# Order of the page, store, gate and head transfers on the issuing queue of a stick-breaking attention stage

## The reference, cut to what matters

```
z = q k^T * SB_HEAD_DIM**-0.5 + bias            # 8 heads of 64
log_keep = where(k_pos < q_pos, log_sigmoid(-z), 0)
between  = reverse_cumsum(log_keep) - log_keep
a = where(k_pos < q_pos, exp(log_sigmoid(z) + between), 0)
o = a v;   o = o * silu(gate)
```

## Time and profile before

| | us |
|---|---|
| median of 3 runs | 3360.61 (3356.51 to 3362.72) |
| the profiled execution | 3363.24 |
| its span | 3360.6 |
| `sb_prompt`, pair 0 (first product to first product of the next) | 574.9 to 670.8 |
| pair 1 | 670.8 to 772.0 |
| pair 2 | 772.0 to 872.8 |
| pair 3, to the last gating | 872.8 to 936.4 |

### The profile page before, as it was taken

How to read it: one execution, slowest core, us unless ns; L and a number is a source line. 1 busy time by engine, 2 the same in 40 slices (tenths; PEclk the granted TensorE clock), 3 DMA queues, 4 the chain that set the end, 5 groups by cost and what they waited for, 6 DMA issues and landing times. The chain is left out here.

```text
span 3360.6 us, 46161 instructions
## 1 busy us (share of the span) xinstructions
PE 2947.2 (88%) x17599; PEld 2570.9 (77%) x17599; DVE 1535.9 (46%) x1933; ACT 861.1 (26%) x1326; POOL 585.4 (17%) x504
## 2 busy tenths in 40 slices
PE   7999998987966888788888999999888998888887
PEld 7988887433436787788568999999777888888657
DVE  6276665777555673341424221111355642341423
ACT  5211113555751101220232100011232232120221
POOL 0002222554711221100011210000222301100011
PEclk9999998867987998899998999999887898989988
DMA  7379886776434002313541222222444453202641
GB/s 262 120 253 308 301 298 205 222 231 200 122 138 163 19 19 80 120 38 121 212 151 50 107 100 100 94 81 100 171 166 143 163 184 104 94 31 99 233 158 63
DMA packets 242194, 489.51 MB, mean 146 GB/s; under 512 B 37897, under 2 KB 98954, under 8 KB 241682
## 3 DMA queue, kind: packets, MB, share of 16 engines
q1 hardware_dynamic: 225298, 429.04, 38.0%
q0 software_dynamic: 12560, 43.07, 3.8%
q10 hardware_dynamic: 4176, 15.32, 1.1%
HBM read 378.83 MB, written 112.78 MB: 146 GB/s over the span
## 5 line engine op out<-in xcount | busy, mean ns | idle before, releaser
L414 PE MATMUL ps<-in_hi,w_hi 128*128 128x344 f32 x2496 | 806.4, 323 | 92.4 <-DVE in_lo L317 92.4
L415 PE MATMUL ps<-in_lo,w_hi 128*128 128x344 f32 x2496 | 803.8, 322 | 0.0
L416 PE MATMUL ps<-in_hi,w_lo 128*128 128x344 f32 x2496 | 802.8, 322 | 0.0
L414 PEld LDWEIGHTS ps<-in_hi,w_hi 128*128 128x128 f32 x2496 | 474.6, 190 | 96.2 <-DVE in_lo L317 96.2
L416 PEld LDWEIGHTS ps<-in_hi,w_lo 128*128 128x128 f32 x2496 | 474.7, 190 | 0.0
L415 PEld LDWEIGHTS ps<-in_lo,w_hi 128*128 128x128 f32 x2496 | 474.6, 190 | 0.0
L273 DVE CAST w_hi<-w_raw 128x1024 fp32r<-128x1024 f32 x64 | 49.5, 774 | 507.8 <-PE ps L416 495.0
L277 POOL TENSOR_TENSOR w_lo<-w_raw,w_hi 128x1024 fp32r<-128x1024 f32 x40 | 95.3, 2388 | 1024.9 <-ACT w_hi L273 1024.9
L1499 PE MATMUL ps<-in_hi,wv_hi 128*128 128x344 f32 x696 | 227.2, 326 | 2.1 <-DVE wv_lo L1349 2.1
L1500 PE MATMUL ps<-in_lo,wv_hi 128*128 128x344 f32 x696 | 223.1, 321 | 0.0
L1501 PE MATMUL ps<-in_hi,wv_lo 128*128 128x344 f32 x696 | 223.1, 321 | 0.0
(11 more groups left out here) (351 smaller groups left out, 5459.4 us busy)
## 6 DMA issues: line engine op xcount, KB each, us to landing
k_pages<-in_cache_k SPq DMA_DIRECT2D x256, 256.0 KB, 4.2
v_pages<-in_cache_v POOLq DMA_DIRECT2D x128, 256.0 KB, 5.1
v_pages<-in_cache_v SPq DMA_DIRECT2D x128, 256.0 KB, 3.0
cc<-stage SPq DMA_DIRECT2D x48, 516.0 KB, 2.7
w_raw<-in_w_c SPq DMA_DIRECT2D x48, 512.0 KB, 4.2
in_raw<-og SPq DMA_DIRECT2D x40, 516.0 KB, 5.6
kq_raw<-in_w_mem SPq DMA_DIRECT2D x32, 512.0 KB, 4.1
xs_kv<-in_mem_k SPq DMA_DIRECT2D x16, 1024.0 KB, 6.7
```

The costliest lines, as they stand in the source:

```text
L414: pe.matmul(o, w_hi[:, u, a:b], h, start=(kt == 0), stop=False)
L415: pe.matmul(o, w_hi[:, u, a:b], l, start=False, stop=False)
L416: return pe.matmul(o, w_lo[:, u, a:b], h, start=False, stop=(kt == KT - 1))
```

## The change

The pages of a group are issued ahead of everything else of that j. The values of the next pair go behind group 1, the store and the gate behind group 2, head 0 behind group 3 and head 1 behind group 4. `prepare` moves from steps 6 and 13 to 14 and 18. The conditions on the pages select the same pages as before, and no transfer or instruction is added or taken out.

```diff
-PREP_AT = (6, 13)
+PREP_AT = (14, 18)
...
             for p in range(PAIRS):
                 for j in range(NJ):
+                    if p + NW + 1 < S:
+                        k_pages(p, j)
+                    if p + NW < S:
+                        v_pages(p, j)
+                    if j == 1 and p + 1 < PAIRS:
+                        sp.wait_ge(vt_done, 2 * p + 2)
+                        sp.dma_start(vt[:, 0:T], ab[AB_V + 1 + p][:, 0:T]).then_inc(v_in, 16)
                     if j == 2:
                         if p:
                             store(p - 1)
                         sp.dma_start(gate[:, :], ab[AB_Z + p][:, 0:T]).then_inc(gate_in, 16)
-                        if p + 1 < PAIRS:
-                            for u in range(2):
-                                load_head(p + 1, u)
-                            sp.wait_ge(vt_done, 2 * p + 2)
-                            sp.dma_start(vt[:, 0:T], ab[AB_V + 1 + p][:, 0:T]).then_inc(v_in, 16)
-                    if p + 1 < PAIRS:
-                        k_pages(p, j)
-                    v_pages(p, j)
+                    if j in (3, 4) and p + 1 < PAIRS:
+                        load_head(p + 1, j - 3)
```

## The result

The changed kernel is slower. Over 20 runs of each its median is 3360.56 us against 3352.93 for the kernel before (the three runs shown ahead of the prediction were among its slower ones); the measured ratio of the two is 1.0027, 95% interval 1.0016 to 1.0037 (it is not simply the quotient of the medians). I had forecast 7 us less; it is some 8 us more.

What follows compares the result with a forecast made beforehand. The prediction took DVE's 26.1 us of waits for late key pages as the bound; 15.6 us gained minus 8.4 for the moved prepares gave 7.2 less, 3353 us, range 3344 to 3364.

Steps and rivals of the forecast that it cites:

- What bounded the stage: DVE at product 2 of each pair with key pages: waits for late K2, 26.1 us in all.
- Group 2 and V2's wait: SP's list: K2 lands early, the 26.1 us go; V2 and all behind it wait for PE's group 0 values.
- K5, the next late page: Product 5: K5 limits the gain to 0.4, 7.3 and 7.9 us in pairs 0, 1, 2, together 15.6.
- as tight as K5, but not tighter: Value pages V4 and V5 on PE: used 3 to 5 us behind products 4 and 5, no limit beyond K5.
- `prepare` at 14 and 18: Late steps of pairs 0 to 2: moved work costs 1.8 us at step 14 plus 6.6 at 18, 8.4 together.
- behind it stands a wait for PE of 2.88 us at step 17, which takes most of that: After step 14: this wait absorbs most of 3.5 us, leaving 0.6 us a pair, 1.8 in all.
- the prediction's own upper end: Steps 14 and 18: the cost of both prepares if no other wait absorbs any, 3 x (3.5 + 2.9) = 19 us.
- the tail of pair 2: Behind step 18: a 2.13 us wait for PE cuts the 2.9 us delay to 0.8.
- The collisions with POOL: Rival: six moved `k_stack` and `q_lo` operations cost 1.22 us each, 7.3 in all; no change, 3361; chance 0.19.
- The rival for slower: Heads delay K5, landing 12.1 us after its first page instead of 7.3; 8.7 us slower, 3369; chance 0.11.

Runs made afterwards that it cites:

- e1: The kernel before with only `prepare` moved from steps 6 and 13 to 14 and 18, queue order old; time 1.0069 of the kernel before.
- e6: The changed kernel with `prepare` at steps 9 and 14 instead of 14 and 18; time 0.9989 of the kernel before.
- e7: The changed kernel with ACT making its copies at steps 13 and 17, DVE's part staying at 14 and 18; time 1.0022 of the kernel before.
- e3: The changed kernel with both heads issued behind group 1 in pairs 1 and 2, `prepare` still at 14 and 18; time 1.0012 of the kernel before.

## Why the prediction was wrong

- **What bounded the stage**: right. Product 2 waits for K2, and K2 is late by its issue and by the data in front of it.
- **Group 2 and V2's wait**: right. The stall at product 2 is gone in all pairs.
- **K5, the next late page**: right in mechanism, some 3 us too favourable. K5 is waited for in each pair; product 5 came 6.7 and 5.7 us earlier in pairs 1 and 2 (7.3 and 7.9 in the sum) and 0.2 later in pair 0 (0.4 earlier). 12.2 of 15.6 us. SP left 1.7 us between gate and K3 where I had 0.78. Against e1, which has the same prepares, the new order is worth 8.9 us of the stage.
- V4 and V5 were to be "as tight as K5, but not tighter". PE waited 16.0 us for values, DVE 13.0 for keys.
- **"`prepare` at 14 and 18", 8.4 us**: the step that failed. The late half grew by 21.2, and e1 puts the price of the late prepares by themselves at 18.0 us of stage. At step 14 the 3.5 us came out as a sum (softplus of step 15 is 3.3 us later) and not in its parts: the wait for ACT's copy is 2.39 us and not 1.03, while before 2.6 us of `prepare` stood in the same stretch. What failed is "behind it stands a wait for PE of 2.88 us at step 17, which takes most of that". The waiting z stands behind the sums of step 16, those behind a `softplus_lo`, that behind the very softplus that `prepare` had delayed. It is a wait in the same loop, and it shifts with it: 2.77 us in e6, 2.98 in e1's pair 1 (2.12 in the changed kernel's, 0.8 less than before). With nothing absorbed the prediction's own upper end was 19, near the 21.2 that came. Instead of 0.6 us a pair product 5 to 7 grew by 2.0 to 3.0.
- The same error stands in the tail of pair 2, where 2.13 us were to absorb most of 2.9. The 2.9 us themselves were right: 2.7, 3.4 and 3.0 in e1. The lower clock of one tail and part of another go with another 4.3 (87.6 against the 83.3 of e1); the prediction had no term for the clock.
- **The collisions with POOL**: right as a mechanism, at the wrong place. The rival priced the six moved operations at 1.22 us each; in the changed kernel POOL had next to nothing to do while they ran (it waits 3.86 us in the row at 739.27), and they took 1.22 to 1.43 us. What collided on the chain is product 6, with a late `softplus_lo` of 3.25 to 3.26 us in each of the three pairs. By the rule of the Trainium skill, page "SBUF — State Buffer", section "SBUF: two separate sides", the loser blocks for the other's instruction: the trace agrees, with 3.26 us for a `softplus_lo` of 1.27 that began 0.14 us after a product of 2.27, and 2.16 for a `k_stack` of 1.22.
- **The rival for slower** named the wrong cause: K5 landed in 7 us, not 12. The sign was not the forecast one.
- The absolute number rested on three runs whose median was 7.7 us above that of twenty. That the time lay within the stated range is luck of these three: as differences from the kernel before the range ran from 16.6 us less to 3.4 more, and the measured one is 7.6 more.

## What to carry to other kernels

A wait absorbs a delay only if what it waits for does not depend on the delayed work. In this kernel's loop over several engines (DVE, ACT, POOL, PE and back) both waits that I had counted on did depend on it; follow the releaser back two or three links before counting on it as cover. When a list of work is moved to make room for late transfers, move the transfers into the queue's idle time first: here that kept the work where it was covered, and made a stage with 26.1 us of page waits 24.2 us shorter.

## What the runs showed of the hardware that I had not expected

- The same 84 rows of PE took 24.0 us at a granted clock of 0.94 and 27.8 at 0.78, and the tail at 0.78 was 3.3 us longer (30.97 against 27.7), in a stage where PE is not the engine that I took for the limit. Waits of 2.5 to 2.9 us on PE were followed by the lower level in some places (0.79 us for the matmul) and not in others (0.50 us), in the same kernel.
- DVE loses to POOL as well: in e7 `k_stack` and `q_lo` took 2.16 and 2.18 us instead of 1.22.
- SP's issuing, 4.41 us for four pages of 256 KB, is a rate limit of this stage by itself: with the heads of pairs 1 and 2 out of its way (e3) PE still waited 16.4 us for values.
